# A hybrid decoder trunk in float32: weight sums of mixer 1 spread out, gate sums and the last FFN's ends moved

## The reference

```python
h = rmsnorm(x, norm1_g) * (1 + sc1) + sh1        # sh1..g2: silu(c) @ ada_w + ada_b
x = x + g1 * hybrid_mixer(h, w_in, ..., w_out)
h = rmsnorm(x, norm2_g) * (1 + sc2) + sh2
x = x + g2 * ((silu(causal_dwconv(gate)) * val) @ w_down)   # gate, val = split(h @ w_up)
return rmsnorm(x, final_g)
```

## Time and profile before

| | us |
|---|---|
| median of 3 runs | 2797.31 |
| lowest, highest | 2796.26, 2800.71 |
| the profiled execution, own time | 2801.3 |
| its span | 2799.5 |
| PE busy | 2713.2 (97%) |
| DVE, POOL, ACT busy | 1836.2, 1100.9, 994.8 |

### The profile page before, as it was taken

One profiled execution on the slowest core, in us unless ns is written; L12 is line 12 of the kernel. 1 busy time (PEld: TensorE's weight loads), 2 busy tenths in 40 slices (PEclk: granted clock), 3 DMA queues, 4 the chain that ended last, 5 costly groups with the idle time before them and its releaser, 6 DMA issues.

```text
span 2799.5 us, 33836 instructions
## 1 busy us (share of the span) xinstructions
PE 2713.2 (97%) x12427; PEld 2214.5 (79%) x12427; DVE 1836.2 (66%) x2589; ACT 994.8 (36%) x1505; POOL 1100.9 (39%) x737
## 2 busy tenths in 40 slices
PE   6999999899999999999999999999999999999997
PEld 6777877678877888877878788888888788887885
DVE  6787955668377566568786565565746754545767
ACT  2544323331153333344535322152224433334333
POOL 3344430555047777644560110001003554444244
PEclk9999999999999999999999999999999999999998
DMA  9678777999755665583448767586675334347545
GB/s 385 228 256 298 254 267 256 345 351 332 261 183 187 208 220 188 185 288 88 162 150 293 235 214 277 179 283 231 220 254 191 122 115 121 127 126 249 180 158 199
DMA packets 262001, 620.49 MB, mean 222 GB/s; under 512 B 26725, under 2 KB 84553, under 8 KB 257739
## 3 DMA queue, kind: packets, MB, share of 16 engines
q1 hardware_dynamic: 261174, 618.08, 64.5%
q10 hardware_dynamic: 662, 0.24, 0.0%
HBM read 466.57 MB, written 151.66 MB: 221 GB/s over the span
## 4 chain that ended last, share of the span: by engine, by line
PE 75%; DVE 8%; DMA 7%; POOL 3%; issue 3%; SPq 2%; ACT 1%; DVEq 0%; ACTq 0%; POOLq 0%
PE main L1956 29%; PE pair L2226 15%; PE main L2226 14%; PE pair L2246 6%; PE main L2246 4%; DMA w_split_scratch<-w_hl 2%; POOL tb L714 2%; PE pair L2093 1%; DMA tb<-in_ff_up_dram 1%; DVE a_lo L1606 1%; DMA t_up_scratch<-tb 1%; POOL w_hl L703 1%; PE pair L2118 1%; DMA w_hl<-w_split_scratch 1%; DVE stats L1167 1%
## 5 line engine op out<-in xcount | busy, mean ns | idle before, releaser
L703 POOL TENSOR_TENSOR w_hl<-w_raw,w_hl 128x512 fp32r<-128x512 f32 x532 | 764.1, 1441 | 904.8 <-ACT w_hl L818 902.8
L818 ACT ACTIVATE w_hl<-w_raw 128x512 fp32r<-128x512 f32 x532 | 332.2, 630 | 802.7 <-PE main L2226 169.3
L1956 PE MATMUL main<-w_hl,h_hi 128*128 128x512 f32 x1536 | 492.3, 401 | 4.8 <-DMA w_hl<-w_split_scratch 4.3
L1956 PEld LDWEIGHTS main<-w_hl,h_hi 128*128 128x128 f32 x1536 | 283.8, 188 | 78.3 <-issue 14.2
L1956 PE MATMUL main<-w_hl,h_lo 128*128 128x512 f32 x768 | 300.2, 391 | 0.0
L751 POOL TENSOR_TENSOR pre_hl<-pre_raw,pre_hl 128x512 fp32r<-128x512 f32 x35 | 53.0, 1518 | 564.2 <-ACT pre_hl L842 564.2
L714 POOL TENSOR_TENSOR tb<-tb,tb 128x512 f32<-128x512 f32 x132 | 209.8, 1590 | 164.8 <-DMA tb<-in_ff_up_dram 160.1
L1956 PE MATMUL main<-h_hi,w_hl 128*128 128x512 f32 x768 | 250.6, 400 | 8.2 <-DMA w_hl<-w_split_scratch 5.8
L1606 DVE TENSOR_TENSOR a_lo<-g,a_hi 128x512 fp32r<-128x512 f32 x132 | 176.8, 1349 | 103.4 <-ACT a_hi L1071 103.1
L2226 PE MATMUL pair<-s_hi,w_hl 128*128 128x512 f32 x736 | 235.6, 393 | 2.4 <-POOL w_hl L703 2.4
L2246 PE MATMUL main<-w_hl,a_hi 128*128 128x512 f32 x704 | 222.1, 397 | 16.1 <-DVE a_lo L1606 12.9
(11 more groups left out here) (281 smaller groups left out, 5115.8 us busy)
## 6 DMA issues: line engine op xcount, KB each, us to landing
w_hl<-w_split_scratch SPq DMA_DIRECT2D x312, 512.0 KB, 4.4
w_split_scratch<-w_hl SPq DMA_DIRECT2D x104, 512.0 KB, 6.7
w_raw<-t_up_scratch SPq DMA_DIRECT2D x176, 256.0 KB, 2.7
w_raw<-in_ff_up_dram SPq DMA_DIRECT2D x132, 256.0 KB, 3.7
tb<-in_ff_up_dram SPq DMA_DIRECT2D x88, 256.0 KB, 4.7
t_up_scratch<-tb SPq DMA_DIRECT2D x88, 256.0 KB, 5.7
g_scratch<-c_val SPq DMA_DIRECT2D x44, 512.0 KB, 4.0
g<-g_scratch SPq DMA_DIRECT2D x40, 512.0 KB, 7.3
```

The lines of the kernel that those rows point to most:

```text
L703: nc.gpsimd.tensor_tensor(w_lo[:, g % RING, :], w_raw[:, g % RING, :], w_hi[:, g % RING, :].bitcast(F32), ALU.subtract).then_inc(w_lo_ok, 1)
L818: nc.scalar.activation(w_hi[:, g % RING, :], w_raw[:, g % RING, :], ACT.Copy).then_inc(w_hi_ok, 1)
L1956: ins = T.matmul(main[i], a, w, start=first and p == 0, stop=last and p == 2)
```

## The change

Ten edits. (1) Prologue: `mod_direct` is split in two, the row transposes come after x's, ACT scales x before it copies columns, and the two halves of the first norm's columns are finished one by one. (2) `mod_column(1, ...)` goes from unit (1, 7) to (2, 2), three units later, and the gate loads wait for it. (3) `GATE_AT` becomes (22, 34, 42, 50, 58, 70, 80, 85). (4) DVE's gate sums move one place later each: pair 4 behind v's scaling, pair 5 behind y's scaling, pair 6 behind yT_lo, pair 7 behind the norm of the next x; PE's gate matmuls go from k = 11 to k = 15 of OUT. (5) The second half of h's transposes goes from k = 7 to 9, and the first four h_lo come ahead of DVE's residual. (6) ACT's evacuation of the first OUT half comes one split earlier. (7) Mixer 1's twenty sum tiles: eight early ones in `tv`, in v's place, every 4.5 units from unit 4, the other twelve every 4 units from 39 to 83. Mixer 1's x2 is loaded three units later. (8) x2's four stores go from units 11 to 14 to 11, 17, 22, 25, h2's from 19 to 22 to 12, 15, 19, 23. (9) `PRE_AT` starts at 30 in steps of 3 instead of 22 in steps of 3.4. (10) In the last FFN POOL does nothing: DVE multiplies by gate and gain (`gate_half`, `gain_left`, `right_scale`) in 128x2048 and 128x512 pieces, with x, g2 and the final gain in h's place (`x_last`, `g2_last`, `fg_last`), and ACT scales only left halves.

```diff
+        tv = [[fixed(f"tv{i}{n}", [P, W], F32, r_at + (48 + 8 * i + 2 * n) * KB)[0] for n in range(4)] for i in range(2)]
...
-        GATE_AT = (20, 34, 42, 50, 58, 68, 78, 84)
+        GATE_AT = (22, 34, 42, 50, 58, 70, 80, 85)
         PRE_OF = {2: range(17), 3: range(17, len(PRE_J))}
-        PRE_AT = [22 + 17 * i // 5 for i in range(18)]
+        PRE_AT = [30 + 3 * i for i in range(18)]
         PRE_BUF = 3
         pre_hi_ok, half_sum, sq_ok = sem("pre_hi_ok"), sem("half_sum"), sem("sq_ok")
+        T_EARLY = 8
         T_OF = (range(0), range(0, 20), range(20, 33))
-        T_AT = ((), [16 + 16 * i // 5 for i in range(20)], [18 + 19 * i // 2 for i in range(13)])
+        T_AT = ((), [4 + 9 * i // 2 for i in range(T_EARLY)] + [39 + 4 * i for i in range(20 - T_EARLY)], [18 + 19 * i // 2 for i in range(13)])
 
         def t_set(t):
             return t % 2 if t < T_OF[2][0] else 1
+
+        def t_buf(t):
+            return tv[t_set(t)] if t < T_EARLY else tb[t_set(t)]
...
-                    sp.wait_ge(mod_col, 1)
+                    sp.wait_ge(mod_col, 2)
...
+            X2_AT, H2_AT = (11, 17, 22, 25), (12, 15, 19, 23)
...
+                                sp.wait_ge(w_used, mix0(b) + RING)
+                            if t == T_EARLY:
                                 sp.wait_ge(x2_st, 16 * NT * b)
                             t_load(t)
-                x2_at_unit = OUT + 17
+                x2_at_unit = OUT + (20 if b == 1 else 17)
...
-                if b == NB:
-                    for step in range(8):
-                        final_step(s, step)
-                    final_gain(s)
...
-            act.wait_ge(col_tr, 2)
-            nc.scalar.activation(col_a[:], aux[0][:, 0:ROWS_A], ACT.Copy).then_inc(col_ok, 1)
-            nc.scalar.activation(col_b[:], aux[0][:, P:P + ROWS_B], ACT.Copy).then_inc(col_ok, 1)
             act.wait_ge(xr_ok, 1)
             for t in range(NT):
                 tile = xn01[:, t, :] if t < 2 else xn23[:, t - 2, :]
                 nc.scalar.activation(tile, tile, ACT.Copy, scale=rstd[:, t:t + 1]).then_inc(xn_ok, 1)
+            act.wait_ge(col_tr, 2)
+            nc.scalar.activation(col_a[:], main[0][:, 0:ROWS_A], ACT.Copy).then_inc(col_ok, 1)
+            nc.scalar.activation(col_b[:], main[0][:, P:P + ROWS_B], ACT.Copy).then_inc(col_ok, 1)
...
-                        if b % 2 == 0 and j == 1 and n in (n0 + LEAD + 1, n0 + LEAD + 7):
+                        if b % 2 == 0 and j == 1 and n in (n0 + LEAD + 1, n0 + LEAD + 9):
...
-                    if j == 0:
-                        evac_to_stage(G_OUT, S_OUT, n0 + 2 * KD - 1, ACT.Copy)
...
+            dve.wait_ge(mod_col, 1)
+            link(V.tensor_tensor(mod_c[:, 0:2 * KD], main[1][:, 0:2 * KD], col_b[:, R_AB:R_AB + 2 * KD], ALU.add))
+            full_at = [acc[:, 0, :], acc[:, 1, :]]
             for half in range(2):
-                mod_columns(0, slice(4 * half, 4 * half + 4), (main[3 - 2 * half], main[2]), R_N1, 1 + half)
-            dve.sem_inc(evacuated, 4)
-            full_at = [acc[:, 0, :], acc[:, 1, :]]
-            h_lows(0, (0, 1), aux, full_at)
+                ks = slice(4 * half, 4 * half + 4)
+                mod_columns(0, ks, main[3 - half], two_parts(mod_c, 0, ks), R_N1, 1 + half)
+                dve.sem_inc(evacuated, 2)
+                if half == 0:
+                    h_lows(0, (0, 1), aux, full_at)
...
-                    if b == 0:
+                    if b == 0 and cc < NT - 1:
...
+                if b == 0:
+                    gate_sums(NT)
...
-                if b == 0:
-                    gate_sums(5)
...
-                    gate_sums(6)
+                    gate_sums(5)
...
-                    gate_sums(7)
+                    gate_sums(6)
                 if b % 2 == 0:
                     norm_x(b + 1, [xnew[:, t, :] for t in range(NT)])
                 if b == 0:
+                    gate_sums(7)
                     dve.wait_ge(pro_dma, 48)
                     for m in range(4):
                         dve.wait_ge(gate_mm, m + 1)
                         row = gate_rows[0:1, m * W:(m + 1) * W]
                         V.tensor_tensor(row, aux[m][0:1, :], row, ALU.add).then_inc(gate_ok, 1)
+                if b == 0:
+                    h_lows(b + 1, range(4), aux, [acc[:, 0, :], acc[:, 1, :]])
...
+                        if (p, k) == (P5, 1):
+                            gate_half(s, 0, 0, 2)
+                        if (p, k) == (P5, 4):
+                            gate_half(s, 1, 0, 8)
+                        if (p, k) == (P5, 5):
+                            add_y(s, 1, 0)
+                        if (p, k) == (P5, 8):
+                            add_y(s, 0, 0)
+                        if (p, k) == (P5, 10):
+                            gain_left(s, 1, NT)
+                        if (p, k) == (P3, 1):
+                            gain_left(s, 0, 2 * NT)
                         if (p, k) == (P3, 5):
-                            dve.wait_ge(pool_fin, s * 6 + 4)
-                            add_y(s, 1, 0)
+                            gate_half(s, 1, 1, 10)
+                        if (p, k) == (P3, 6):
+                            add_y(s, 1, 1)
                         if (p, k) == (P3, 7):
-                            dve.wait_ge(pool_fin, s * 6 + 6)
-                            add_y(s, 1, 1)
+                            gate_half(s, 0, 1, 12)
                         if (p, k) == (P3, 8):
-                            dve.wait_ge(pool_fin, s * 6 + 8)
                             add_y(s, 0, 1)
...
+            def gate_half(s, half, c, after):
+                cols = slice(c * W, (c + 1) * W)
+                dve.wait_ge(g2y_in, 16 * (s + 1))
+                dve.wait_ge(d_add, s * (12 + NT) + after)
+                yy = y_half[half][:, :, cols]
+                link(V.tensor_tensor(yy, yy, g2_last[:, cols].unsqueeze(1).broadcast_to([P, NT, W]), ALU.mult))
...
+            def right_scale(half):
+                for t in range(NT):
+                    xx = x_of(NSB - 1, half)[:, t, W:D]
+                    V.scalar_tensor_tensor(out=xx, in0=xx, scalar=rstd[:, 4 * half + t:4 * half + t + 1], in1=fg_last[:, W:D],
+                                           op0=ALU.mult, op1=ALU.mult).then_inc(half_sum, 1)
...
-            mod_direct(main[2])
-            pe.wait_ge(rows_in, 176)
-            T.transpose(aux[0][:, 0:ROWS_A], rows_a[0:ROWS_A, :], ident[0:ROWS_A, 0:ROWS_A]).then_inc(col_tr, 1)
-            T.transpose(aux[0][:, P:P + ROWS_B], rows_b[0:ROWS_B, :], ident[0:ROWS_B, 0:ROWS_B]).then_inc(col_tr, 1)
-            pe.wait_ge(col_ok, 2)
+            mod_direct(main[1], range(KD))
             pe.wait_ge(xn_ok, NT)
             h_transpose(0, range(4), xn, aux)
+            pe.wait_ge(rows_in, 176)
+            T.transpose(main[0][:, 0:ROWS_A], rows_a[0:ROWS_A, :], ident[0:ROWS_A, 0:ROWS_A]).then_inc(col_tr, 1)
+            T.transpose(main[0][:, P:P + ROWS_B], rows_b[0:ROWS_B, :], ident[0:ROWS_B, 0:ROWS_B]).then_inc(col_tr, 1)
+            mod_direct(main[1], range(KD, 2 * KD)).then_inc(mod_col, 1)
             pe.wait_ge(ada_summed, KD - ADA_PE)
             mod_column(0, range(4), main[3])
-            mod_column(0, range(4, KD), main[1])
+            mod_column(0, range(4, KD), main[2])
...
-                        if b == 0 and (j, k) == (1, 7):
+                        if b == 0 and (j, k) == (2, 2):
...
-                        if b == 0 and j == 0 and k == 11:
+                        if b == 0 and j == 0 and k == 15:
...
-                        if b % 2 == 0 and j == 1 and k in (1, 7):
+                        if b % 2 == 0 and j == 1 and k in (1, 9):
```

More of the change, by code:

```diff
@@ L344, in hybrid_decoder_trunk, with x_of @@
         assert all(g % RING == i % RING for g, i in PRE_G.items())
+        def x_of(s, half):
+            return x_last if half and s == NSB - 1 else x_half[half]
         def loaded(g):
@@ L706, in t_step @@
             def t_step(t, step):
-                b11, b21, b12, b22 = (tile[:] for tile in tb[t_set(t)])
+                b11, b21, b12, b22 = (tile[:] for tile in t_buf(t))
                 if step == 0:
@@ L971, in mixer @@
                             nc.scalar.activation(arow[:], arow[:], ACT.Exp).then_inc(exp_ok, 1)
+                    if b == 1 and cc == 2:
+                        for m in range(2):
+                            act.wait_ge(t_st[m], 64 * len([t for t in range(T_EARLY) if t_set(t) == m]))
                     for i in range(4):
@@ L990, in mixer @@
                     for n in range(n0 + LEAD, n0 + 2 * KD + LEAD):
+                        if j == 0 and n == n0 + 2 * KD + LEAD - 1:
+                            evac_to_stage(G_OUT, S_OUT, n0 + 2 * KD - 1, ACT.Copy)
                         split(mix0(b) + n)
@@ L1874, in finish0 @@
                 dve.wait_ge(xr_ok, NSB + 1)
-                dve.wait_ge(fg_in, 16 * (s + 1))
-                for t in range(NT):
-                    xx = x_half[0][:, t, W:D]
```

(3 more changed lines are left out.)

129 lines of the change are left out of this document (67 added, 62 removed).

## The result

The changed kernel takes 2811.74 us (median of 5 runs, 2808.69 to 2816.41) against 2797.95 for the kernel before (5 runs, 2796.26 to 2800.98): ratio 1.0047, 95% interval 1.0035 to 1.0059. It is slower by about 13 us, half a per cent, where 14.5 us less were forecast, and it lies outside the range.

The account below looks back on a forecast made before the run. PE was taken as busy for 2713.2 of 2799.4 us, leaving at most 86.2 us of waits; eight terms summed to -14.5 us, from 2801.3 profiled to 2786.8, carried to the median as 2782.8, range 2756 to 2794.

Parts of the forecast that it names:

- Weight sums in mixer 1: Start of mixer 1: respaced tiles and stores keep SyncE from standing, so loads come less late: -8.0 us.
- Rival B: Mixer 1 becomes bound by transfers, its 34 MB passing no faster than today: +10 or +25 us there; chance 0.08.
- Prologue: Start of the kernel: unit 0 starts near 40.0 instead of 46.3: -6.3 us.
- SyncE at unit 80: OUT of mixer 0: loads wait for gate sums behind y's scaling, so PE starts unit 80 late: +14.3 us.
- SyncE at unit 89: OUT of mixer 0: x2's load waits for the later gate matmuls, delaying weights and the first outputs' evacuation: +8.9 us.
- Rival A: SyncE's stops at units 80 and 89 are covered, so both costs fall away: 2759.6 us; chance 0.26.
- h2's columns: Mixer 0, at 101.52: PE's wait for a weighted sum mostly becomes one for da_t: -0.6 us.
- Gate sums one slot later: Mixer 0: PE's wait for y's scaling goes and a pair no longer stands ahead of v's scaling: -3.7 us.
- h's second transposes: End of mixer 0: transposes no longer wait for DVE's low tiles, and slow clock behind them goes: -5.6 us.
- The end: Last FFN: with GpSimd idle, PE runs product P3's eleven units without a wait: -13.5 us.
- Rival C: Last FFN: DVE becomes the bound, its 128x2048 operations staying at 4.49 us: -5.5 for -13.5, 2790.8 us; chance 0.14.
- rival D: Prologue and mixer 1 give half and both SyncE stops stay: 2792.5 us; chance 0.05.

Follow-up runs that it names:

- x7: The changed kernel with mixer 1's sum tiles, x2 load and x2's and h2's stores as before the change: 2801.44 us, ratio 1.0002.
- x4: The changed kernel with each store of a mixer 1 sum tile six units after its load instead of four: 2794.13 us, ratio 0.9982.
- x6: The kernel before with the new prologue alone: 2801.85 us, ratio 1.0007.
- x10: Change with gate sums, loads and matmuls as before, tile stores six units after load, weights of units 4 to 7 ahead of modulation columns: 2772.15 us.
- x1: The changed kernel with gate sum pairs 4 to 7, gate loads from unit 68 on and gate matmuls as before: 2791.68 us, ratio 0.9975.
- x5: x1 with the gate matmuls at k = 15 again, as in the change: 2801.16 us, ratio 0.9998.
- x11: x10 with the fourth pair of gate sums behind v's scaling and its loads at unit 70: 2769.49 us, ratio 0.9895.
- x3: The kernel before with only the new end of the last FFN: 2787.68 us, ratio 0.9952.
- x13: Change with old prologue, gate sums, loads and matmuls as before, tile stores six units after load: 2772.53 us, ratio 0.9904.

## Why the prediction was wrong, and where it was right

The prediction was wrong in the sign of the whole. Two of its eight terms failed, one was too small, and five held. The step that decided the sign is the first below.

- *Weight sums in mixer 1, -8.0.* This is the step that failed: +12.6 by x7, +10.3 in the traces. I wrote that "a store is followed by the load that needs its buffer five units later, so SyncE does not stand there". It does not stand at that load, but it stands at the store itself, for POOL's sums, which I did not count: the store was left four units after the load, and load, landing and four sums take longer than four units here (11.7 us against 10.9 in the tile above). That put SyncE's waits for POOL at 104.6 us, where they were 40.0. Rival B named the side but not the cause, since the transfers were not the bound: x4 moves the same bytes and gains 18 us. Most of the forecast gain comes with x4: its mixer 1 is 12.6 - 18.2 = -5.6 us against before, and -6.6 in the traces (309.1 against 315.7). The mistake was to price the wait that the change removes and not to ask, of the same queue, what its other waits then are.
- *Prologue, -6.3.* Unit 0 came at 39.93, forecast near 40.0, by the steps given. But x6 shows +2.0 (-1 to +5), not -6.3. I had it as a bound ("0, if weights or h's last tile keep the old pace") with the DMA share of 0.96 beside it, and took the other end without following the queue past 50 us, where ACT's splits at 66 and 68 wait for SyncE's transfers. x10 shows that their order is a part of it; what the rest is stays open.
- *SyncE at unit 80, +14.3.* Right. Its cause is at hand in the trace: ACT's next split is one that waits 16.93 us for SyncE's transfers; the row names the store of the slot's earlier weights, held back as the load is. PE reached unit 80 11.7 us late by the ledger (-4.8 to +6.9), forecast 11.8, though two steps in it were off in opposite directions: SyncE went on at 334.77 (forecast 339.0, it needed only the first of the pair's sums) and the weights then took longer, 13.5 us to the second instead of 11.5. The 11.5 was itself counted from the end of both sums, 322.2; by the same reading as here, from SyncE's loads at 321.06, it was 12.6. The runs show this stop only together with the moved gate sums (-3.7 below): 10.6 to 13.7 us by times, 10.1 in the traces, where the two terms make 14.3 - 3.7 = 10.6.

```profile
334.77 1.52 SPq L449 DMA_DIRECT2D mod_sum<-in_ada_w_dram  x2
...
345.13 0.63 ACT L827 ACTIVATE w_hl<-w_raw 128x512 fp32r<-128x512 f32 x1 [16.93 <-DMA w_split_scratch<-w_hl]
348.28 0.63 ACT L827 ACTIVATE w_hl<-w_raw 128x512 fp32r<-128x512 f32 x1 [2.52 <-DMA w_split_scratch<-w_hl]
```

- *SyncE at unit 89, +8.9.* Right: 6.4 to 9.5, and 7.1 in the traces. From x2's load to the split 6.9 us (forecast 6.65), from there to PE another 1.3; PE's wait was 8.18 us. Rival A, that the ring covers the stops, falls by x1 and x5.

```profile
380.62 0.33 SPq L560 DMA_DIRECT2D x<-in_x_dram  x1
...
387.50 0.63 ACT L827 ACTIVATE w_hl<-w_raw 128x512 fp32r<-128x512 f32 x1 [14.59 <-DMA w_split_scratch<-w_hl]
```

- *h2's columns, -0.6.* The new wait for da_t is there, 2.77 us, but the ledger gains 3.7 between dt's products and 127.40: the slow clock behind the old wait went too, which I had only as the far bound. The one pair of traces overstates it: between these two places the four kept traces with the old order need 48.5 to 52.2 us (mean 50.7), the ten with the new one 48.3 to 50.0 (mean 48.8), so about 2 us. No run tests it alone.
- *Gate sums one slot later, -3.7.* In the ledger -2.7 to the first y transposes; the wait for y is gone. Over the kept traces this stretch takes 206.2 to 208.5 us in the four with the sums moved and 210.4 to 213.8 in the nine with the sums in their old places, 4.6 less on average. Its price was the stop at 80, so the pair should not be moved: x1 takes all moves back and gains; x11 keeps the one pair (v's) that stops nobody.
- *h's second transposes, -5.6.* From +16.9 at the unit before which they stood to +10.9 at mixer 1's first unit: -6.0. From OUT's second half to mixer 1 the four kept traces with the old order take 51.9 to 53.1 us, and the five with the new one and no stop at 89 take 47.1. Read from traces, not tested alone.
- *ACT's evacuation one split earlier* had no term of its own. From unit 80 to OUT's second half these same four and five traces take 27.1 to 27.5 us and 25.6, and PE's wait of 1.38 is gone: about -1.5, not tested alone.
- *The end, -13.5.* Right in size and in steps: -13.4 by both traces and by x3. P3 ran from 2764.37 to 2794.46, 30.1 us, as eleven units of 2.72; PE has no wait in the last 64 us, and 12.5 us followed (forecast 12.6). Rival C falls: 2.28 us per operation with GpSimd idle.

```profile
2764.37 0.62 PE L2287 MATMUL main<-w_hl,a_hi 128*128 128x512 f32 x2
...
2794.07 0.39 PE L2287 MATMUL main<-w_hl,a_lo 128*128 128x512 f32 x1
```

The forecast's sum with the two failed terms replaced by what x6 and x7 measured is -14.5 + 8.3 + 20.6 = +14.4, and the change measured +13.8. That it comes so near is partly luck, as both replacements are uncertain by some 3 us (mixer 1's is 10.3 in the traces, not 12.6). The range missed it because mixer 1 growing had a chance of 0.08 there, and because I priced that by bandwidth, the one way in which it did not grow. Two of the forecast's figures do not follow from its own words: rival D, with half the gain of prologue and mixer 1, is 2782.8 + 7.2 = 2790.0 and not 2792.5; and the parts named under *Numbers* add up to 0.75 for faster, 0.19 for the same and 0.05 for slower, not 0.84, 0.10 and 0.06.

By the Trainium skill, "HBM Reference", section "Specifications (TRN2)", a core that streams alone goes above the 358 GB/s that I took from "DMA: Bandwidth & Descriptors" as what HBM gives one core. The 377 GB/s of the first 50 us and fortieths of x4's stretch from 437 to 770 at up to 410 GB/s agree; a ceiling of 358 is not what these stretches show.

## What to carry to other kernels

When waits in an in-order queue are moved, follow every wait of every moved step, not the one that the move is meant to remove: a buffer cycle has a gap from load to store and one from store to reload, and each must be longer than what it covers at the load the DMA engines then have. Work brought forward ahead of a stretch that is fed by full DMA engines gave nothing here (x6, x13); look 30 us further for the transfer that fixes the time. Taking work from GpSimd while DVE adds two operands paid here although DVE then did the work itself (x3), and its size could be read from one row with GpSimd idle and one with it busy.

## What the runs showed of the hardware that was not expected

- One unit more between a tile's load and its store (2.7 us) took SyncE's waits for POOL from 104.6 us to 5.3 and the kernel down by 17 to 19 us; a second one changed nothing (2795.16 and 2794.13).
- The same one-line edit that takes 18 us off the change adds 51 to the kernel before: the ring of two tile sets has no slack on one side or the other.
- One load of raw weights, unit 8's, took SyncE 9.17 us to issue in the change, right behind 50 us in which the DMA engines' share is 0.97; where little is in flight the same instruction takes 0.33. Before the change it began 5.6 us later and took 3.69 (first row the change, second before):

```profile
49.03 9.17 SPq L394 DMA_DIRECT2D w_raw<-in_w_in_dram  x1
...
54.61 3.69 SPq L382 DMA_DIRECT2D w_raw<-in_w_in_dram  x1
```

Both issues end at the same time, 58.2 and 58.3. So SyncE came to this load earlier and was done with it no earlier, and the next load follows at 59.6 in both; this is where the prologue's gain was lost. Why an issue takes so long the profile does not show.
